# Causal masks of the mixers: added in place by VectorE instead of multiplied in by TensorE

## The reference, cut to what matters

```python
causal = k_pos[None, :] <= q_pos[:, None]
s_f = jnp.einsum('bhqd,bhkd->bhqk', qf, k_f).astype(jnp.float32) * scale_f
s_f = s_f + cf[..., :, None] - cum_f[..., None, :]
s_f = jnp.where(causal, s_f, -jnp.inf)
p_f = jax.nn.softmax(s_f, axis=-1)
o_f = jnp.einsum('bhqk,bhkd->bhqd', p_f.astype(v_f.dtype), v_f)
s_d = jnp.einsum('bhcqd,bhckd->bhcqk', qd, k_d).astype(jnp.float32) * scale_d
s_d = jnp.where(causal, s_d, -jnp.inf)
p_d = jax.nn.softmax(s_d, axis=-1)
a_d = p_d[:, :, 0] - lam * p_d[:, :, 1]
o_d = jnp.einsum('bhqk,bhkd->bhqd', a_d.astype(v_d.dtype), v_d)
```

## Time and profile before

| | us |
|---|---|
| median of three runs | 2626.52 |
| profiled execution | 2627.89 |
| its span | 2626.1 |
| TensorE busy | 2610.0 (99%) |
| VectorE busy | 1419.7 (54%) |
| ScalarE busy | 1023.2 (39%) |
| GpSimd busy | 227.6 (9%) |

### The profile page before, as it was taken

How to read it: one execution, slowest core, us unless ns; L and a number is a source line. 1 busy time by engine, 2 the same in 40 slices (tenths; PEclk the granted TensorE clock), 3 DMA queues, 4 the chain that set the end, 5 groups by cost and what they waited for, 6 DMA issues and landing times.

```text
span 2626.1 us, 33116 instructions
## 1 busy us (share of the span) xinstructions
PE 2610.0 (99%) x12382; PEld 2131.5 (81%) x12382; DVE 1419.7 (54%) x1861; ACT 1023.2 (39%) x1588; POOL 227.6 (9%) x164
## 2 busy tenths in 40 slices
PE   8999999999999999999999999999999999999999
PEld 7888888878888888888887778888887888888777
DVE  5444248875444235444258765444236657845773
ACT  4222135654222233222145653223135553334663
POOL 0000024101000010000033111000000000012220
PEclk9999999999999999999999999999999999999999
DMA  4222233113222223222232112222222222322221
GB/s 164 96 96 96 96 104 97 65 41 105 96 96 98 99 90 102 98 97 96 96 111 82 58 64 96 96 96 96 96 88 81 78 83 85 109 93 93 84 70 56
DMA packets 70323, 239.13 MB, mean 91 GB/s; under 512 B 8528, under 2 KB 10832, under 8 KB 70224
## 3 DMA queue, kind: packets, MB, share of 16 engines
q1 hardware_dynamic: 69792, 236.91, 27.1%
q10 hardware_dynamic: 432, 0.87, 0.1%
HBM read 230.15 MB, written 2.10 MB: 88 GB/s over the span
## 4 chain that ended last, share of the span: by engine, by line
PE 92%; DVE 3%; issue 2%; ACT 1%; DVEq 0%; POOL 0%; DMA 0%; POOLq 0%; ACTq 0%; SPq 0%
PE bank L410 21%; PE bank L412 20%; PE bank L411 20%; PE score L411 5%; PE score L410 5%; PE score L412 5%; PE flip_bank L410 2%; PE flip_bank L411 2%; PE flip_bank L412 2%; PE score L1140 1%; PE flip_bank L1168 1%; PE bank L2697 1%; PE score L2665 1%; PE score L1857 1%; PE bank L1190 1%
## 5 line engine op out<-in xcount | busy, mean ns | idle before, releaser
L393 DVE TENSOR_TENSOR w_lo<-w_raw,w_hi 128x1024 fp32r<-128x1024 f32 x427 | 525.8, 1233 | 537.3 <-ACT w_hi L353 526.5
L410 PE MATMUL bank<-h_hi,w_hi 128*128 128x512 f32 x1856 | 740.5, 399 | 1.1 <-DVE w_lo L393 1.1
L412 PE MATMUL bank<-h_hi,w_lo 128*128 128x512 f32 x1856 | 724.4, 390 | 0.0
L411 PE MATMUL bank<-h_lo,w_hi 128*128 128x512 f32 x1856 | 723.3, 390 | 0.0
L353 ACT ACTIVATE w_hi<-w_raw 128x1024 fp32r<-128x1024 f32 x427 | 447.8, 1051 | 396.3 <-DMA w_raw<-stream 396.0
L410 PEld LDWEIGHTS bank<-h_hi,w_hi 128*128 128x128 f32 x1856 | 349.1, 188 | 75.8 <-issue 5.0
L412 PEld LDWEIGHTS bank<-h_hi,w_lo 128*128 128x128 f32 x1856 | 348.8, 188 | 73.7
L411 PEld LDWEIGHTS bank<-h_lo,w_hi 128*128 128x128 f32 x1856 | 349.4, 188 | 71.8 <-issue 2.4
L539 ACT ACTIVATE hid_hi<-tmp 128x512 f32 (+1 forms) x88 | 55.6, 632 | 409.7 <-DVE tmp L753 409.7
L747 DVE TENSOR_TENSOR tmp<-bank,rstd 128x512 f32<-128x512 f32 x132 | 91.1, 691 | 147.2 <-PE bank L412 146.9
L534 ACT ACTIVATE tmp<-tmp 128x512 f32<-128x512 f32 x88 | 55.6, 632 | 247.7 <-DVE tmp L747 247.7
(11 more groups left out here) (516 smaller groups left out, 3819.5 us busy)
## 6 DMA issues: line engine op xcount, KB each, us to landing
w_raw<-stream SPq DMA_DIRECT2D x427, 512.0 KB, 3.2
tmp<-tmp SPq DMA_DIRECT2D x64, 64.0 KB, 2.1
x_tok<-x SPq DMA_DIRECT2D x4, 512.0 KB, 6.7
wx_raw<-stream SPq DMA_DIRECT2D x4, 512.0 KB, 4.7
out<-out_tok SPq DMA_DIRECT2D x8, 256.0 KB, 2.0
tmp<-qr SPq DMA_DIRECT2D x16, 64.0 KB, 2.7
tab_in_f<-tables SPq DMA_DIRECT2D x1, 704.0 KB, 10.4
cos_sin<-rope ACTq DMA_DIRECT2D x1, 512.0 KB, 5.0
```

What stands on the lines that cost most here:

```text
L393: nc.vector.tensor_tensor(w_lo[:, s, :], w_raw[:, s, :], w_hi[:, s, :].bitcast(F32), ALU.subtract).then_inc(lo_ready, 1)
L410: nc.tensor.matmul(dst, whi, xhi, start=start, stop=False)
L411: nc.tensor.matmul(dst, whi, xlo, start=False, stop=False)
L412: return nc.tensor.matmul(dst, wlo, xhi, start=False, stop=stop)
```

## The change

The 128 mask products (L1146) go. On VectorE `maxima(k)` gets a `tensor_tensor` add in front of the maximum, in place on `score`, with the same bf16 table read again for each bank. At b = 0 one add covers four diagonal blocks (blocks 0 and 1 of both banks), 512 elements a partition; at b = 2 and b = 3 one add covers two, 256 elements; at b = 1 there is none. A `drain` stands between the add and the maximum. So a group has 3 adds and a mixer 24, 48 in all. In differential groups the last score product now signals `scored`. In gated groups the mask comes after the forget sums instead of ahead of them.

```diff
--- before.py
+++ after.py
@@ -840,7 +840,17 @@
                                             ALU.subtract).then_inc(v_ready, 1)
 
                 def maxima(k):
+                    b = STEPS[k][1]
                     dve.wait_ge(scored, NSTEP * layer + k + 1)
+                    if b == 0:
+                        diagonal = score[:, :, :].rearrange("p c (t n) -> p c t n", n=2 * P)[:, :, :, 0:P]
+                        causal = table_b("causal").unsqueeze(1).unsqueeze(1).broadcast_to([P, 2, 2, P])
+                    else:
+                        diagonal = score[:, :, P * b:P * b + P]
+                        causal = table_b("causal").unsqueeze(1).broadcast_to([P, 2, P])
+                    if b != 1:
+                        nc.vector.tensor_tensor(diagonal, diagonal, causal, ALU.add)
+                        dve.drain()
                     nc.vector.tensor_reduce(softstat[:, 2 * k:2 * k + 2, 0], score[:, :, score_cols(STEPS[k][1])], AX_X,
                                             ALU.max, negate=True).then_inc(maxed, 1)
 
@@ -1137,14 +1147,10 @@
                         for e in blocks:
                             for c in range(2):
                                 rows = slice(HEAD * c, HEAD * c + HEAD)
-                                nc.tensor.matmul(score[:, c, score_cols(e)], q[rows, g % 2, P * e:P * e + P],
-                                                 kk[rows, g % 2, 0:P * (e + 1)],
-                                                 start=q is q_hi and kk is k_hi and e == blocks[0], stop=False)
-                    for c in range(2):
-                        for e in blocks:
-                            end = score_cols(e).stop
-                            ins = nc.tensor.matmul(score[:, c, end - P:end], table_b("identity"), table_b("causal"),
-                                                   start=False, stop=is_diff(g) and e == blocks[-1])
+                                ins = nc.tensor.matmul(score[:, c, score_cols(e)], q[rows, g % 2, P * e:P * e + P],
+                                                       kk[rows, g % 2, 0:P * (e + 1)],
+                                                       start=q is q_hi and kk is k_hi and e == blocks[0],
+                                                       stop=is_diff(g) and q is q_lo and e == blocks[-1])
                     if not is_diff(g):
```

## The result

The changed kernel takes 2634.03 us (median of 9 runs, 2632.71 to 2636.19) beside 2627.5 us of the kernel before on the same chip (9 runs, 2625.72 to 2631.46): 6.5 us more, ratio 1.0026 [1.0017, 1.0035]. The forecast was 2632.5. The span of its profiled execution is 2632.2 us beside 2626.1.

The account below looks back on a forecast made before the run. TensorE was taken to bound the kernel (busy 2610.0 of 2626.1 us), with VectorE bounding the dense stretch after the change. Lateness of +3.0 us a mixer, +6.0 for two, takes the median from 2626.5 to 2632.5; range 2626.5 to 2641.

Parts of the forecast that it names:

- The price of an add: On VectorE, each add delays the maximum 0.77 us at b = 0, 0.49 at b = 2 and 3: 14 us a mixer.
- The fourth rival: Mixers: GpSimd holds the adds, +2 to +4 us a mixer on top, 2637 to 2641, up to 2650; chance 0.17.
- The credit of TensorE: TensorE without mask products wins 4.4 us a mixer; 3.6 if no switch is won, 5.2 if both are.
- Steps 0 to 5: Start of a mixer: two adds leave TensorE 0.55 us early (S = -0.55) instead of 0.94.
- Steps 6 to 15: Dense stretch, 438 to 491 us: eight adds, 4.48 us, partly absorbed by idle time; TensorE's lateness taken as S = +2.5.
- Steps 16 to 31: After the dense stretch: TensorE wins 1.76 us, four places lack slack; lateness ends at S = +3.0.
- the waits at steps 23, 24, 28 and 31: Four places without slack, waiting on exponentials or a key's low half; waits at 24 and 28 grow by about 0.5 us.
- Two mixers: Both mixers, the second having the same rows as the first: +6.0 us in all.
- feed-forward stages and the second network keep their lengths: Sign of a right forecast: the parts outside the mixers stay as long as before.
- The signs: In 438 to 491: no VectorE idle over 0.3 us, about 3 us longer; TensorE waits about 9 to 10 a mixer.
- The first (credit kept): Mixers: the adds' lateness is hidden and TensorE keeps its credit, about -1.7 to -4.4 us, 2618 to 2623; chance 0.08.
- the second (idle time used): Mixers: cheap adds and idle time used up, S between -1 and +2.5 us a mixer, 2625 to 2631.5; chance 0.32.

Follow-up runs that it names:

- e1: The changed kernel without its adds, so neither mask products nor adds and the mixers' attention unmasked: 2621.94 us beside 2626.83 before, ratio 0.9979.
- e2: The kernel before with the adds put in and the 128 mask products kept: 2640.16 us beside 2626.83 before, ratio 1.0052.
- e4: The kernel before with the change in the differential groups alone (steps 0 to 15), gated groups keeping the product: 2632.52 us beside 2626.83, ratio 1.0021.
- e3: The kernel before with the change in the gated groups alone (steps 16 to 31), differential groups keeping the product: 2627.87 us beside 2626.83, ratio 1.0003.
- e6: The kernel before with the change only at b = 0 of the gated groups (8 of 48 adds): 2625.85 us beside 2627.29, ratio 0.9993.
- e10: The kernel before with adds replacing products only at nine steps a mixer that traces showed with slack: 2625.07 us beside 2627.29, ratio 0.9993.
- e7: The changed kernel with `flip_low(k - 2)` (`pt_lo`) called ahead of add and maximum instead of behind: 2641.63 us beside 2627.03 before, ratio 1.0058.
- e5: The changed kernel with each add and its drain issued twice: 2656.95 us beside 2627.03 before, ratio 1.0111.

## Why the prediction was right, and where its sizes were off

**The price of an add** held. VectorE's groups by shape, 406 to 592 us, changed kernel, columns as in the earlier trace rows:

```profile
L852 DVE TENSOR_TENSOR score<-score,tabb 128x256 f32<-128x256 f32 x16 | 6.8, 423 | 4.2 <-PE score L1150 2.4 <-PE score L1160 1.8
...
L852 DVE TENSOR_TENSOR score<-score,tabb 128x512 f32<-128x512 f32 x8 | 5.5, 693 | 2.1 <-PE score L1160 1.9
```

693 and 423 ns beside the 687 and 412 of the subtraction taken for it. The successor starts 0.76 and 0.50 after the add (0.77 and 0.49 forecast), as the timeline of VectorE shows at one place of each size:

```profile
427.43 0.69 DVE L852 TENSOR_TENSOR score<-score,tabb 128x512 f32<-128x512 f32 x1
428.19 0.42 DVE L854 TENSOR_REDUCE softstat<-score 128x2 f32<-128x256 f32 x1
...
437.37 0.43 DVE L852 TENSOR_TENSOR score<-score,tabb 128x256 f32<-128x256 f32 x1 [1.60 <-PE score L1150]
437.87 0.96 DVE L854 TENSOR_REDUCE softstat<-score 128x2 f32<-128x768 f32 x1
```

**The fourth rival** (adds held by GpSimd) fell: none of the 48 lasts over 700 ns, though GpSimd is busy 18.74 of the 53 us. Three adds of the first mixer run wholly beside instructions of GpSimd and last 680, 412 and 431 ns. The Trainium skill (GPSIMD Engine Reference, Specifications) names the instructions with two SBUF inputs or in a two-port mode as those that contend, and the adds have one input in PSUM; the trace agrees. Other rows are stretched in the changed kernel, but not the same ones as before:

```profile
439.54 1.22 DVE L393 TENSOR_TENSOR w_lo<-w_raw,w_hi 128x1024 fp32r<-128x1024 f32 x1
...
442.20 1.49 DVE L869 SCALAR_TENSOR_TENSOR probs<-probs,softstat 128x384 f32<-128x384 f32 x1
```

The same two in the kernel before:

```profile
439.63 2.26 DVE L393 TENSOR_TENSOR w_lo<-w_raw,w_hi 128x1024 fp32r<-128x1024 f32 x1
...
443.33 0.62 DVE L859 SCALAR_TENSOR_TENSOR probs<-probs,softstat 128x384 f32<-128x384 f32 x1
```

1.04 less in the first and 0.87 more in the second: where such rows fall can move a stretch by about a microsecond. From the maximum of step 6 to that of step 16 the rows of VectorE other than the adds sum to 54.94 us before and 55.97 in the changed kernel.

**The credit of TensorE** was a term that was off in size. The rows of the changed kernel, steps 0 and 6, beside the earlier trace rows:

```profile
407.42 0.39 PE L1150 MATMUL score<-k_hi,q_lo 64*128 64x128 f32 x4
407.75 0.50 PE L410 MATMUL bank<-h_hi,w_hi 128*128 128x512 f32 x1
...
436.99 0.34 PE L1150 MATMUL score<-k_hi,q_lo 64*128 64x384 f32 x2
437.25 0.50 PE L410 MATMUL bank<-h_hi,w_hi 128*128 128x512 f32 x1
```

I took one of two changes of operands as won. None is: the projection behind the score products has a row of 0.50, no less than the 0.47 behind the mask, and starts 0.33 after the last scores where the mask product did (0.32). So a differential group wins 0.20 + 0.10 + 0.10 = 0.40, not 0.65, and a mixer 4 x 0.40 + 4 x 0.44 = 3.4 us, not 4.4. The lower end of 3.6 was added up wrong: 4.4 less twelve changes of 0.08 is 3.4, and that is what came. The 81 ns a pair of the Trainium skill (TensorE: Matmul & The Clock Gate, Back-to-back issue gap) would put it higher still; the row disagrees.

The next three paragraphs follow the lateness of TensorE in the first mixer, as the forecast did (negative means early).

**Steps 0 to 5.** Forecast -0.55. Step 6's scores start at 436.53 beside 436.91, -0.38, or about -1.0 against the first product, of which 0.44 stood already when step 0 began (406.86 beside 406.71, less the 0.6 of the start). So the steps themselves brought about -0.5. The 0.44 are no gain of the change: the same stretch ahead of step 0 is about 0.5 shorter or longer in the other kernels too (-0.50 in e1, +0.56 in e2).

**Steps 6 to 15.** Forecast +3.05 (from -0.55 to +2.5); measured 59.80 us from step 6's scores to step 16's beside 55.32, so +4.5. This is the step that was sized too low. VectorE's idle time was reckoned to take up 0.8 of the adds; the growth is as large as the 4.48 of adds in full. VectorE idled again for 0.16 and 0.61 us in the window and 0.59 behind it, at waits for copies and exponentials that themselves came later, and its other rows took 1.0 us more, so how much of the idle time helped can't be told apart. In the second mixer the same stretch (1406.41 to 1462.53 before, 1410.93 to 1470.18 now) grew from 56.12 to 59.25, by 3.1, which is the forecast's size: the step failed in one mixer of two. e4 puts nearly the whole loss here, too.

**Steps 16 to 31.** Forecast +0.5 (2.5 to 3.0); measured 4.1 to 5.0, +0.9, with the waits at steps 23, 24, 28 and 31 as named; they grew by 0.60, 0.65, 0.43 and 0.41 where about 0.5, 0.5, 0.44 and 0.32 were said. e3, with 12 adds here and none ahead, comes out at +1.0 over two mixers.

**Two mixers.** +4.4 and +3.6 instead of 3.0 each, 8.0 in all at the end of the second, without the 0.6 at the start; at the end of the span 5.5 are left. The 2.5 us come back in the second network, outside the change, in two parts. TensorE's waits for the low half of the weights fell from 2.1 to 1.2 us there, so 0.9. And the granted clock fell once in the profiled execution of the kernel before and not in that of the changed one. The windows of that place (the clock is the third column from the end), before and then now, where TensorE comes there about 8 us later:

```profile
2435.00:2445.00 10.00, 10.00 (x51) 8.39 (x51) 7.86 (x17) 3.96 (x9) 0.00 (x0) 0.83 0.25 79
```

```profile
2443.00:2453.00 10.00, 10.00 (x57) 8.40 (x56) 7.46 (x16) 4.98 (x10) 0.85 (x1) 1.00 0.26 80
```

That is 10 x 0.17 = 1.7 us, and TensorE's lateness drops from 7.6 to 6.1 across it. It goes with the execution and not with the change, as far as the runs tell: six of the twelve profiled executions have this fall, those of before, e1, e2, e3, e6 and e10, and among the runs of the kernel before alone the mean granted clock is 1.000 in some and 0.999 in others. So the forecast's "feed-forward stages and the second network keep their lengths" is not quite right. The mixers cost 2 us more than the forecast's 6.0 and about 1 came back outside; that the median (+6.5) meets it so closely is in part one error against another.

**The signs.** The stretch of the dense window grew by 4.5 and 3.1 us, not 3. VectorE has one idle time of 0.61 us there, where none over 0.3 was said. The waits were said to sum to 9 to 10 us a mixer; they are 13.7 for both, 7.0 in the first. An idle time isn't all that a wait costs, though: a row lasts 0.39 and its neighbour starts after 0.23, so by an estimate from these rows each wait costs 0.16 more than it shows. With all waits but the first (6.2 us before, 16.5 after) and 14 more of them: 10.3 + 14 x 0.16 - 2 x 3.4 = 5.7. The spans without the 0.6 at the start and without the clock's 1.7 are 7.2 apart. For e7 (all waits 21.4 us, 18 more of them, 1.7 by its own clock) the same sum gives 15.2 + 18 x 0.16 + 1.7 - 6.8 = 13.0 beside 14.3 by the same measure, and for e2 9.1 beside 11.9 (both executions have the fall in the second network). So 1.3 to 2.8 us of each are not in the waits as they are summed here, and stay open.

**The rivals.** The first (credit kept) and the second (idle time used) end at or below 2631.5 and are out: all nine runs of the changed kernel took longer (2632.71 at the lowest), and in e1, where the credit comes alone, the kernel is faster, so it is the adds that take the credit back.

## What to carry to other kernels

Before work goes from the busiest engine to another, look at the stretch and not at the average: VectorE was 54% busy over the program and 94% in the 53 us that counted, and most of what the change cost came from there (+5.7 of 6.5 by e4), while as many adds in the other half, with their credit, cost +1.0. Price the moved work where it lands, ahead of whom in the queue; and don't count a credit of the bounding engine if it then waits for the engine that was given the work. What comes out of a stream of products is worth its start-to-start spacing, with no change of operands credited unless a row shows it.

## What the runs showed of the hardware

- A change between 64-row score products and 128-row projections costs 0.08 to 0.11 us, whether 0.2 us of bf16 products stand between or not.
- Four bf16 products of 128 columns took 0.21 us of TensorE's time, though each row reads 219 ns.
- An add in place in PSUM with a bf16 operand in SBUF (693 ns for 512 elements, 423 for 256) costs VectorE as much as a subtraction from PSUM to SBUF; GpSimd's work beside it didn't stretch it (680, 412 and 431 ns where it ran all the time).
- The granted clock of a mixer fell to 0.50 for 3.4 us twice in e5, once some 2 us behind an idle time of TensorE of 1.75 us and once some 1 us behind one of 1.84, and once in e7, some 1 us behind an idle time of 0.32 that had one of 1.17 just ahead of it. The length of an idle time alone doesn't decide it: idle times of 1.79 (e5, ending at 501.38 us), 1.85 (e5, at 546.48) and 2.13 (e7, at 467.88) were followed by 1.00 for at least 8 us.
- In the second network the clock fell to 0.50 for 3.4 us in six of the twelve profiled executions, 2.4 to 3.1 us behind an idle time of only 0.35 to 0.39; behind that idle time stand eight products of one column each (the kernel before: at 2437.80). The changed kernel passes the same place at 1.00.
